# Tile one's ranks and its half of the first expert gather moved ahead of tile two's selection; VectorE applies tile two's root and bias; the last copy of x goes in halves

## What is computed

```python
x = layer_norm(DN_ALPHA * x + merged @ w_o[i], ln1_g[i], ln1_b[i])
y_m = hier_moe(x, w_grp[i], b_grp[i], w_exp[i], b_exp[i], w_gate[i], w_up[i], w_down[i])

# hier_moe, cut to what matters
grp_logits = xt @ w_grp + b_grp
g_top = jnp.argmax(grp_logits, axis=-1)                 # one of 8 groups
exp_logits = jnp.einsum('td,dge->tge', xt, w_exp) + b_exp
sel = exp_logits of group g_top                         # 8 experts
top_vals, top_idx = lax.top_k(sel, 2)
weights = p_g[:, None] * jax.nn.softmax(top_vals, axis=-1)
expert_id = g_top[:, None] * 8 + top_idx                # 2 of 64 experts for each token
# each expert: silu(x w_gate) * (x w_up) @ w_down on its tokens; weighted sum per token
```

## Time and profile before

| | |
|---|---|
| median of 3 runs | 1563.42 us (1559.3 to 1564.12) |
| profiled execution | 1566.86 us |
| its span in the trace | 1564.8 us |
| TensorE matmul busy | 1302.7 us, 83% |
| VectorE, ScalarE, GpSimd busy | 423.0, 206.1, 33.7 us |
| DMA | 503.85 MB, mean 322 GB/s |

### The profile page before, as it was taken

One profiled execution on the slowest core, in us unless ns is written; L12 is line 12 of the kernel. 1 busy time (PEld: TensorE's weight loads), 2 busy tenths in 40 slices (PEclk: granted clock), 3 DMA queues, 4 the chain that ended last, 5 costly groups with the idle time before them and its releaser, 6 DMA issues.

```text
span 1564.8 us, 21667 instructions
## 1 busy us (share of the span) xinstructions
PE 1302.7 (83%) x8729; PEld 730.4 (47%) x8729; DVE 423.0 (27%) x817; ACT 206.1 (13%) x401; POOL 33.7 (2%) x92
## 2 busy tenths in 40 slices
PE   9999999996576677578999999998767658757787
PEld 4686444553233434234466854455534425424433
DVE  4344442511010011111634464344101101101126
ACT  2311000211010000000213120012101100000011
POOL 2000000100000000000100000001000000000000
PEclk9999999998788798889999999999978978978898
DMA  9733467499999999999674344657999999999990
GB/s 315 264 108 109 163 255 306 172 425 425 426 426 424 425 424 426 427 426 418 230 275 162 108 145 166 258 210 297 424 426 427 426 425 422 425 426 427 427 383 27
DMA packets 105225, 503.85 MB, mean 322 GB/s; under 512 B 15155, under 2 KB 18245, under 8 KB 55109
## 3 DMA queue, kind: packets, MB, share of 16 engines
q1 hardware_dynamic: 104564, 501.85, 79.7%
q10 hardware_dynamic: 592, 1.06, 0.2%
HBM read 501.83 MB, written 1.05 MB: 321 GB/s over the span
## 4 chain that ended last, share of the span: by engine, by line
PE 58%; DMA 37%; DVE 2%; issue 2%; SPq 1%; ACT 0%; POOL 0%; ACTq 0%; POOLq 0%; DVEq 0%
DMA ring<-in_w_down 36%; PE ps L1219 11%; PE ps L992 9%; PE ps L688 7%; PE ps L758 7%; PE ps L1039 5%; PE ps L703 5%; PE ps L1164 3%; PE ps L1183 3%; PE ps L1232 1%; SPq L516 1%; DMA ring<-in_w_in 1%; PE ps L1313 0%; PE ps L1123 0%; PE ps L835 0%
## 5 line engine op out<-in xcount | busy, mean ns | idle before, releaser
L1219 PE MATMUL ps<-ring,pads 128*32 128x512 f32 x384 | 167.1, 827 | 113.8 <-DMA ring<-in_w_down 113.8
L1219 PE MATMUL ps<-scratch,pads 128*32 128x512 f32 x512 | 167.1, 791 | 89.1 <-DMA ring<-in_w_down 88.9
L1183 PE MATMUL ps<-ring,pads 128*32 128x256 f32 x2560 | 227.0, 379 | 0.0
L1183 PEld LDWEIGHTS ps<-ring,pads 128*32 128x32 f32 x2560 | 121.9, 110 | 75.6 <-issue 11.5
L1164 PEld LDWEIGHTS ps<-pads,xT 128*128 128x128 f32 x1024 | 124.6, 200 | 27.0 <-issue 27.0
L1164 PE MATMUL ps<-pads,xT 128*128 128x128 f32 x1024 | 125.5, 283 | 10.3 <-issue 10.3
L1232 PE MATMUL ps<-mats,pads 128*128 128x512 f32 x256 | 118.3, 605 | 2.4 <-ACT mats L1503 2.4
L2072 DVE COPY mats<-ps 128x512 f32<-128x512 f32 x32 | 22.1, 692 | 358.5 <-PE ps L1219 358.5
L1219 PEld LDWEIGHTS ps<-ring,pads 128*32 128x32 f32 x384 | 37.6, 146 | 169.9 <-issue 124.8
L1183 PE MATMUL ps<-scratch,pads 128*32 128x256 f32 x1536 | 116.2, 379 | 0.0
L758 PE MATMUL ps<-ring,xT 128*128 128x512 f32 x256 | 112.4, 593 | 0.0
(11 more groups left out here) (295 smaller groups left out, 1216.6 us busy)
## 6 DMA issues: line engine op xcount, KB each, us to landing
ring<-in_w_up SPq DMA_DIRECT2D x128, 1024.0 KB, 25.9
scratch<-in_w_gate SPq DMA_DIRECT2D x96, 1024.0 KB, 25.8
scratch<-in_w_down SPq DMA_DIRECT2D x64, 1024.0 KB, 21.6
ring<-in_w_in SPq DMA_DIRECT2D x48, 1024.0 KB, 7.2
ring<-in_w_down SPq DMA_DIRECT2D x48, 1024.0 KB, 23.2
ring<-in_w_gate SPq DMA_DIRECT2D x32, 1024.0 KB, 26.0
x<-in_w_down SPq DMA_DIRECT2D x16, 1024.0 KB, 26.3
ring<-in_w_br SPq DMA_DIRECT2D x12, 1024.0 KB, 6.2
```

Of the source, the lines that this page charges most:

```text
L1183: ins = mm(ps[32 * j:32 * j + 32, 2, i * 256:i * 256 + 256], xgT[:, k, 32 * j:32 * j + 32], w[j][:, k, :], start=(k == 0), stop=(k == K - 1))
L1219: ins = mm(ps[32 * j:32 * j + 32, n, :], hT[:, cc, 32 * j:32 * j + 32], w[j][:, cc, n * 512:n * 512 + 512], start=(cc == 0), stop=(cc == 1))
```

## The change

- TensorE: the rank products of tile one go into `wo11` after slice 6 (`rank_of_first_tile`): one 128x64 product, and one of 128x128 that fills the second and third block of 64 columns at once. Tile one's eight products of the first gather go behind `begin_acc(0)` (`gather_of_first_tile`). The two keep-clock matmuls are dropped. After tile two's selection there remain two rank products, `begin_acc(1)`, and the eight products of tile two's gather, which wait for the low and the high half of the copy separately.
- VectorE: after tile one's selection it makes tile one's ranks and its half of the first `Psel`. After tile two's selection it applies root and bias of tile two (one 128x1024 instruction), then makes tile two's ranks and half of `Psel`.
- ScalarE: no scaling of tile two any more. Tile one's permuted copy goes ahead of the copy of tile two's first transposes; tile two's goes in halves of four slices, each with its own semaphore; the load into `XSLOT` waits for the second.
- GpSimd: no bias any more.
- Memory: tile two's transposed values go to `pads` and the selection's temporary to the scratch area; tile two's logits are in the second bank of the pair of `rank`, and the job `logit1` is gone.

```diff
-IDLE = {"first LayerNorm": 3, "first x": 1, "first xT": 1, "router": 2, "second LayerNorm": 6}
+IDLE = {"first LayerNorm": 3, "first x": 1, "first xT": 1, "router": 0, "second LayerNorm": 6}
-        x1T = [xT[:, :, 0:128], v2(oM, K, 128)]
+        x1T = [xT[:, :, 0:128], pads[:, 0:1024].rearrange("p (k n) -> p k n", k=K)]
@@ SyncE
                 elif slot == XSLOT:
-                    once(sp, "xp_ready", L)
+                    once(sp, "xp_high_ready", L)
                     once(sp, "acc_begun", L)
@@ GpSimd
-                    if i == 0:
-                        bias_of_second_tile(L)
@@ TensorE
+                def rank_of_first_tile():
+                    start_job("rank", L)
+                    once(pe, "asg0_ready", L)
+                    r = half("rank", 0)
+                    mm(r[:, 0:NE], tri[:, :], asg[:, 0, :], start=True, stop=True, skip_group_check=True)
+                    mm(r[:, NE:3 * NE], ones[:, :], asg[:, 0, :].unsqueeze(1).to_broadcast([128, 2, NE]),
+                       start=False, stop=False, skip_group_check=True).then_inc(first_rank, 1)
-                tm_quarter("wo11", wo, xT, L, 1, 1, lambda: mixed_transposes(1, 0))
+                tm_quarter("wo11", wo, xT, L, 1, 1, {3: lambda: mixed_transposes(1, 0), 6: rank_of_first_tile})
                 begin_acc(0)
+                def gather_of_first_tile():
+                    wait_read(pe, "logit0", L)
+                    pe.wait_ge(first_P, L + 1)
+                    once(pe, "xp0_ready", L)
+                    for k in range(K):
+                        mm(ps[:, k // 4, (k % 4) * 128:(k % 4) * 128 + 128], xT[:, k, 0:128], Psel[0][:, 0, :],
+                           start=(k % 4 == 0), stop=False, skip_group_check=True)
+                gather_of_first_tile()
                 once(pe, "asg_ready", L)
-                mm(r[:, 0:NE], tri[:, :], asg[:, 0, :], start=True, stop=True)
-                mm(r[:, NE:2 * NE], tri[:, :], asg[:, 1, :], start=True, stop=False)
-                mm(r[:, NE:2 * NE], ones[:, :], asg[:, 0, :], start=False, stop=True)
-                mm(r[:, 2 * NE:3 * NE], ones[:, :], asg[:, 0, :], start=True, stop=False)
-                ins = mm(r[:, 2 * NE:3 * NE], ones[:, :], asg[:, 1, :], start=False, stop=True)
+                mm(r[:, NE:2 * NE], tri[:, :], asg[:, 1, :], start=False, stop=True, skip_group_check=True)
+                end_job("rank", mm(r[:, 2 * NE:3 * NE], ones[:, :], asg[:, 1, :], start=False, stop=True,
+                                   skip_group_check=True))
                 begin_acc(1).then_inc(ev["acc_begun"], 1)
+                def gather_of_second_tile(c):
+                    pe.wait_ge(P_ready, c)
+                    once(pe, "xp_ready", L)
+                    for k in range(K):
+                        if k == 4:
+                            once(pe, "xp_high_ready", L)
+                        ins = mm(ps[:, k // 4, (k % 4) * 128:(k % 4) * 128 + 128], xT[:, k, 128:256], Psel[0][:, 1, :],
+                                 start=False, stop=True, skip_group_check=True)
@@ first section: instead of gather(c0 + 1, 0)
+                        gather_of_second_tile(c0 + 1)
+                        wait_read(pe, "rank", L)
@@ ScalarE
                 mixed_copy(0, 1)
+                wait_full(act, "logit0", L)
+                permuted(0, 0, K).then_inc(ev["xp0_ready"], 1)
                 mixed_copy(1, 0)
-                permuted(0)
                 mixed_copy(1, 1)
-                act.mul(x[:, 1, :], x[:, 1, :], rstd[:, 1:2]).then_inc(scaled, 1)
...
-                permuted(1).then_inc(ev["xp_ready"], 1)
+                act.wait_ge(second_logits, L + 1)
+                permuted(1, 0, 4).then_inc(ev["xp_ready"], 1)
+                permuted(1, 4, K).then_inc(ev["xp_high_ready"], 1)
@@ VectorE
                 select(0)
+                once(dve, "asg0_ready", L)
+                rank(0)
+                one_hot(0, slice(0, 4), 0).then_inc(first_P, 1)
                 residual(1, 1)
                 moments(1)
                 centre_and_gain(1)
                 select(1)
+                scale_and_bias(1)
+                once(dve, "asg_ready", L)
+                rank(1)
+                one_hot(1, slice(0, 4), 0).then_inc(P_ready, 1)
```

More of the change, by code:

```diff
@@ L761, in tm_quarter @@
                         flush(ins)
-                    if between is not None and k == K // 2 - 1:
-                        between()
+                    if between is not None and k in between:
+                        between[k]()
                 end_job(name, ins)
@@ L1098, in logits @@
                     wait_read(pe, f"x1T{t}_{('lo', 'hi')[n]}", L)
-                    if n == 0:
-                        start_job(f"logit{t}", L)
+                    if (t, n) == (0, 0):
+                        start_job("logit0", L)
+                    out = half("logit0", 0) if t == 0 else half("rank", 1)
                     for k in range(4 * n, 4 * n + 4):
-                        ins = mm(half(f"logit{t}", 0)[:, 0:NLG], x1T[t][:, k, :], wr[:, k, :],
-                                 start=(k == 0), stop=(k == K - 1))
+                        ins = mm(out[:, 0:NLG], x1T[t][:, k, :], wr[:, k, :], start=(k == 0), stop=(k == K - 1))
                         if k == 0:
                             flush(ins)
-                    if n == 1:
-                        end_job(f"logit{t}", ins)
+                    if (t, n) == (0, 1):
+                        end_job("logit0", ins)
+                    elif n == 1:
+                        ins.then_inc(second_logits, 1)
+                def rank_of_first_tile():
[5 more added lines that the diff above has]
+                       start=False, stop=False, skip_group_check=True).then_inc(first_rank, 1)
                 def first_tile_mixed():
@@ L1149, in _ @@
-                wait_read(pe, "rank", L)
-                once(pe, "xp_ready", L)
                 def slot_of(s, n, arrived, count, step):
@@ L1255, in section @@
                     c0 = L * ALLG + s0
+                    first = s0 == 0
                     def turn(uu, c, step, last=False):
@@ L1271, in turn @@
                             combine(c + 1)
-                    gather(c0 + 1, 0)
+                    if first:
+                        gather_of_second_tile(c0 + 1)
+                        wait_read(pe, "rank", L)
+                    else:
+                        gather(c0 + 1, 0)
                     gate_up(s0, landed, "land", first=True, taken=c0 + 1)
@@ L1940, in select @@
                 def select(t):
-                    name = f"logit{t}"
-                    wait_full(dve, name, L)
                     dve.wait_ge(power_out, power(L, "ln1", t))
-                    done(name, dve.scalar_tensor_tensor(lg[:, t, :], half(name, 0)[:, 0:NLG], rstd[:, t:t + 1], br[:, :],
-                                                        ALU.mult, ALU.add))
-                    wait_read(dve, name, L)
+                    if t == 0:
+                        wait_full(dve, "logit0", L)
+                        done("logit0", dve.scalar_tensor_tensor(lg[:, 0, :], half("logit0", 0)[:, 0:NLG], rstd[:, 0:1],
+                                                                br[:, :], ALU.mult, ALU.add))
+                        wait_read(dve, "logit0", L)
+                    else:
+                        dve.wait_ge(second_logits, L + 1)
+                        link(dve.scalar_tensor_tensor(lg[:, 1, :], half("rank", 1)[:, 0:NLG], rstd[:, 1:2],
+                                                      br[:, :], ALU.mult, ALU.add))
                     alone(dve)
@@ L1967, in select, with rank, one_hot @@
                                                    ALU.is_equal, ALU.add)
+                    signal(("asg0_ready", "asg_ready")[t], ins)
+                def rank(t):
                     if t == 0:
-                        link(ins)
+                        dve.wait_ge(first_rank, L + 1)
                     else:
-                        signal("asg_ready", ins)
+                        wait_full(dve, "rank", L)
+                    link(dve.scalar_tensor_tensor(rankx[:, t, 0:NE], half("rank", 0)[:, t * NE:t * NE + NE], 1.0,
+                                                  asg[:, t, :], ALU.add, ALU.mult))
+                    link(dve.tensor_scalar(rankx[:, t, 0:NE], rankx[:, t, 0:NE], 1.0, None, ALU.subtract))
+                def one_hot(t, col, pb):
+                    o = Psel[pb][:, t, :].rearrange("p (j r) -> p j r", j=4)
+                    iota_b = iota[:, 0:32].unsqueeze(1).to_broadcast([128, 4, 32])
+                    return dve.tensor_tensor(o, rankx[:, t, col].unsqueeze(2).to_broadcast([128, 4, 32]), iota_b,
+                                             ALU.is_equal)
                 residual(0, 0)
@@ L2012, in weigh_P @@
                     ins.then_inc(weights_ready, 1)
-                build_P(slice(0, 4), 0, L * ALLG + 1)
                 once(dve, "etop_ready", L)
```

64 lines of the change are left out of this document (25 added, 39 removed).

## The result

The changed kernel takes 1551.04 us (median of 5 runs, 1550.87 to 1553.06), the kernel before 1563.42 (1559.07 to 1564.96): 12.4 less by the medians. The ratio is 0.9936, with an interval from 0.9922 to 0.9949, which is 8.0 to 12.2 us less. The forecast was 1550.5, or 12.9 less: 0.5 from the median, but 0.7 outside the ratio's interval, whose centre is 10.0 less.

A forecast was written before the change was run, and what follows sets the result against it. The unbroken expert-weight stream, opened by gate_up(0), was taken as the bound. Rank, selection, scaling, begin_acc(1) and gather terms gave 6.3 and 6.6 us a layer, together 12.9: 1550.5 us against the median, range 1546.5 to 1557.5.

The forecast's parts named there:

- What bounds it: Both layers: everything after the router is tied to gate_up(0)'s start; the gain per layer is the microseconds that start moves.
- Two rank matmuls in `wo11`: Output projection before the router: tile one's two rank matmuls, placed after the seventh slice, add 0.45 us to the path.
- GpSimd: Tile two's selection: without GpSimd's bias, VectorE's 128x64 tensor_tensor drops from 2.28 to 0.27, -2.01 us.
- VectorE's own scaling: After tile two's selection: VectorE applies root and bias itself in a 128x1024 instruction of 1.28, +1.3 us on the path.
- The rank products: TensorE after tile two's selection: the rank products from 296.69 to 299.09 leave the path, -2.4 us.
- `begin_acc(1)` and the clock: TensorE before the gather: at full clock begin_acc(1) takes 1.77 instead of 3.52, -1.75 us.
- The rival that the clock falls: Router: TensorE's clock still falls to half, losing 3.2 a layer; 1553.7 for one layer, 1556.9 for both; chance 0.14.
- The gather: Before gate_up(0): only tile two's 8 products stay on the path, 1.90 instead of 3.80, -1.9 us.
- The sum: gate_up(0) starts 6.3 us earlier in layer one and 6.6 in layer two, together 12.9.
- Is the DMA side ready: Before the unbroken stream: queue dry about 304.2, first load issued at 304.0, just in time, still a short stop.
- The allowance of 0.6 a layer: DMA queue ahead of the unbroken stream: 0.6 us a layer allowed at the low end.
- The step from the trace to the median: Whole kernel: gain of 12.9 taken off the profiled 1566.86 gives 1554.0, moved down by 3.44 to 1550.5 against the median.

The follow-up runs named there:

- e2: Kernel before, with ScalarE's scale and GpSimd's bias removed and VectorE applying tile two's root and bias after the selection; 1554.55 us, ratio 0.9950.
- e3: Changed kernel with ScalarE's scale and GpSimd's bias of tile two put back and VectorE's scaling of tile two out; 1557.64 us, ratio 0.9964.
- e1: Kernel before with five keep-clock matmuls in the router instead of two, nothing else; 1557.55 us, ratio 0.9971.
- e10: Changed kernel with tile one's eight gather products moved back behind begin_acc(1) and no keep-clock products; 1559.04 us, ratio 0.9970.
- e9: Changed kernel with tile one's eight gather products moved back behind begin_acc(1) and three keep-clock products in the gap; 1555.32 us, ratio 0.9948.
- e4: Changed kernel with four extra 128x512 identity products between the first gather and gate_up(0); 1557.96 us, ratio 0.9969.
- e7: Changed kernel with VectorE scaling tile two in two halves, begin_acc(1) starting with the first and handing over the ring slot with its second product; 1552.58 us, ratio 0.9939.
- e8: Changed kernel with wo11 handing over its four ring slots one by one instead of all behind wo11; 1552.93 us, ratio 0.9937.
- e5: Changed kernel run again unchanged, on the same chip as the three that follow; 1551.85 us, ratio 0.9935.
- e11: Changed kernel with tile two's permuted copy in one piece instead of halves; 1552.08 us, ratio 0.9928.

## Why the prediction was right, and where it was not

**What bounds it** held. In every trace the stretch from the first waiting `w_down` to the last landing of the first half of the experts is that of before within 1 us in either layer. Of the 13.5 by which the two spans differ, 12.3 are there at the last such landing of layer two; the other 1.2 lie in the stretch behind it, which no edit touches and which takes 275.0 to 277.3 in the fourteen traces, with the kernel before at the upper end.

**Two rank matmuls in `wo11`**, +0.45 forecast. From the start of `wo11`'s second half to the residual it is 3.92, before 3.56: +0.36. VectorE's one-hot ends at the very moment at which the residual starts (287.76), and the chain runs through VectorE's three new instructions and not through the end of `wo11`: the price comes by another way than the 0.45 of TensorE that I had added, though the two are close to a tie, which I had seen.

**GpSimd**, -2.01 forecast: the row went from 2.28 to 0.27, and e2 and e3 show cause and effect in both directions. The whole stretch from the residual to what follows tile two's selection (TensorE's rank products before, VectorE's scaling now) went from 9.51 to 7.33, that is -2.18.

**VectorE's own scaling**, +1.3: 1.29, and 0.14 more to TensorE's start, so +1.42 from start to start. **The rank products** took 2.40 off the path, as forecast.

**`begin_acc(1)` and the clock**, -1.75: 3.52 became 1.96, so -1.56. It takes 1.77 in e1, where it follows other products without a gap; I had taken that price for a start out of idleness. The rival that the clock falls, with its chance of 0.14, did not come; e10 shows what kept it away: with a gap of 2.45 the clock fell. The Trainium skill, "TensorE: Matmul & The Clock Gate", "What's actually happening", calls the throttled state the default and says that activity releases it; the traces agree, since tile one's gather kept the clock at 1.00 where the two keep-clock products of the kernel before had not, and it does work besides.

**The gather**, -1.9: 3.80 became 1.78, so -2.02; e9 confirms the size with 1.8.

**The sum.** `gate_up(0)` moved by 6.74 and 7.05 from the residual, less 0.36 and 0.37 for the residual's own delay: 6.4 and 6.7, together 13.1 where 12.9 was forecast. The terms' errors (+0.19 on `begin_acc(1)` and +0.12 on the scaling; -0.17, -0.12 and -0.09 on selection, gather and `wo11`) are small and cancel in part.

**Is the DMA side ready** is the step that was mis-sized. I had the queue dry at 304.2, with a stop of 1 us behind it. It was moving the last load until about 305, and no stop followed. I had counted 2.46 for each megabyte and nothing for the change from one load to the next. The window of the changed kernel at the end of the four `w_up` loads, where the windows before 299.5 have 393 GB/s or more:

```profile
299.50:300.00 0.50, 0.50 (x7) 1.00 0.62 148
```

With 246 GB/s from 300 to 300.5 this is about half a microsecond lost. The allowance of 0.6 a layer was short in layer one: the last landing in the first half of the experts is 211.0 after `gate_up(0)`, and 210.0 to 210.2 in before and e1 to e4, so about 1.0 was taken back there; in layer two the delay of 0.5 was gone by that point.

**The step from the trace to the median** is the other weak one, and the near hit of the median is in part luck. I took a gain worked out on the profiled execution and subtracted it from the median of the runs. But that execution is the slowest that there is of the kernel before (1566.86, mean granted clock 0.917). The 47 runs of it that stood beside the experiments, by their mean granted clock:

| mean granted clock | runs | us | median us |
|---|---|---|---|
| 0.917 to 0.919 | 19 | 1560.26 to 1566.59 | 1564.4 |
| 0.920 | 22 | 1559.07 to 1564.47 | 1562.2 |
| 0.921 to 0.924 | 6 | 1558.69 to 1560.51 | 1560.0 |

Half clock for 6.5 us in each of two layers is 13 of 1565 us at half speed, which takes 0.004 off the mean clock: an estimate from the earlier trace rows, and about the distance between the first and the last row. So the half clock, worth 3.0 and 3.3 a layer in e1's trace, seems to be shorter or absent in some runs of the kernel before, as in e3; no trace of such a run was kept, so this is argued and not shown. The changed kernel's five runs all have 0.921 to 0.923 and lie within 2.2 us. It would explain why the times of before, e1 and the changed kernel differ by less than their traces: e1's centre is 4.5 less where the trace has 6.4, and the change's centre is 10.0 less where the two moves make 13.1. The median of five, 12.4 less, is the number that happens to be near to the forecast. (A slip without weight: the low end of the range, 1546.5, is 2.8 below 1549.3, where half the spread of 4.8 would be 2.4.)

**What stays open.** Why a landing is late: the 28 landings show that late ones occur only with the early `gate_up(0)`, not by what mechanism, and e7 and e8 speak against the overlap of loads as the whole reason. And how much the noise hides: the time from the last landing of layer one's first half to the next layer's residual is 539.9 to 542.2 in the fourteen traces, though the edits touch in it only what stands around `wo11`, and tile two's residual in layer one comes at 289.41 in e7's trace where the others have 287.0 to 287.8. I estimate from this that medians cannot tell less than about 1.5 us here, which leaves e5, e7, e8 and e11 alike.

## What to carry to other kernels

When a stream of loads runs without a break, look for the instruction that opens it, and count the change in the microseconds by which that instruction moves; ask at once whether the queue will be empty when it does, because transfers that ended 2 us ahead of the opener may still be running when it comes 6 us earlier. Compare several runs before taking a gain off a median: the execution that was profiled may be the slowest of them, and a clock that falls may not fall in each run. Fill a gap of TensorE with work that is waiting anyway, before filling it with matmuls for the clock; and if no such work is at hand, three products for the clock were worth 3 us a layer here. A large elementwise instruction on GpSimd can stop VectorE's smallest one: look at the longest instance of a form, not at its mean.

## What the runs showed of the hardware

- A 128x64 tensor_tensor on VectorE took 2.27 to 2.35 beside a 128x1024 tensor_tensor on GpSimd, and 0.27 without it, in both layers of all fourteen traces. The other way round GpSimd's root of one column took 1.46 beside VectorE's 1.28 instruction (tile two), and 0.58 with VectorE idle (tile one), in before and in the changed kernel. The root of tile two is on the chain, so up to 0.9 us a layer may be left there; no run tried it.
- TensorE's clock stayed at 1.00 over idle times of 0.67 and 0.63 with 0.66 of work between them, and over one of 0.80 (e2). It fell to 0.50 with idle times of 2.45 (e10) and 2.79 (before, where it fell during the idle time itself). It can fall when the engine is at work again: in e10 work resumed at 295.06, with 0.63 idle before 296.35, and the clock fell at 297; it was at 1.00 again from 300.5.
- A load issued into an idle DMA queue moved its first data 0.5 to 1.2 us later and reached 400 GB/s 2.0 to 2.7 us later (issued at 287.32, 301.00 and 310.29 in the kernel before, seen in half-microsecond windows). The change from the four `w_up` loads to the next cost about half a microsecond although the queue was never empty (148 and 246 GB/s from 299.5 to 300.5 in the changed kernel).
